# The rows that a piece of a DRAM-to-DRAM table copy takes: 128 in one stretch, or every 128th

## What is computed

```python
q = (ht @ w_q).reshape(-1, PEER_HEADS, PEER_QDIM)
s1, s2 = ...                                  # scores against two sets of 128 sub-keys
best, pos = lax.top_k(cand, PEER_TOPK)        # 8 heads x 16 experts
idx = jnp.take_along_axis(cidx, pos, axis=-1)
u = jnp.take(expert_u, ib, axis=0)            # rows of 1024 float32, 4 KB
act = jax.nn.gelu(jnp.einsum('td,tkd->tk', hb, u))
vrows = jnp.take(expert_v, ib, axis=0)
y = jnp.einsum('tk,tkd->td', gb * act, vrows)
```

## Time and profile before

| what | us |
|---|---|
| median of three runs (lowest, highest) | 4177.75 (4168.81, 4183.3) |
| the profiled execution | 4131.7 |
| its span in the trace | 4129.9 |
| last stage (gathers from `uv_d`), from about 1794 | some 2336 of the span |
| copy in stage A / B / E / S / P | 26 to 157 / 222 to 304 / 392 to 447 / 502 to 595 / 1241 to 1587 |
| TensorE, VectorE, GpSimd busy | 80%, 59%, 43% |
| bytes moved by DMA | 1563 MB, 378 GB/s over the span |

### The profile page before, as it was taken

How to read it: one execution, slowest core, us unless ns; L and a number is a source line. 1 busy time by engine, 2 the same in 40 slices (tenths; PEclk the granted TensorE clock), 3 DMA queues, 4 the chain that set the end, 5 groups by cost and what they waited for, 6 DMA issues and landing times.

```text
span 4129.9 us, 32128 instructions
## 1 busy us (share of the span) xinstructions
PE 3298.1 (80%) x8957; PEld 1643.4 (40%) x8957; DVE 2455.5 (59%) x4977; ACT 1088.2 (26%) x2932; POOL 1769.1 (43%) x1588
## 2 busy tenths in 40 slices
PE   8775589999928878749779779878878977977776
PEld 5453256666524444324224323323323423422222
DVE  0122168998857677544864764674684585485454
ACT  2102011111113233213333333333333333323322
POOL 1020137787723333114444454444444444445554
PEclk9876799999958888969999999999999999999999
DMA  9898899999999998469999999999999999999998
GB/s 352 297 290 310 321 304 413 411 407 414 412 360 341 344 354 300 160 269 420 421 421 418 415 420 399 421 414 409 420 409 409 419 417 403 422 406 422 422 422 353
DMA packets 303586, 1563.05 MB, mean 378 GB/s; under 512 B 31280, under 2 KB 59184, under 8 KB 179888
## 3 DMA queue, kind: packets, MB, share of 16 engines
q0 software_dynamic: 228096, 1300.34, 78.7%
q1 hardware_dynamic: 60736, 239.86, 15.0%
q10 hardware_dynamic: 14592, 21.10, 1.4%
HBM read 1517.54 MB, written 179.04 MB: 411 GB/s over the span
## 4 chain that ended last, share of the span: by engine, by line
DMA 26%; PE 18%; issue 7%; DVE 4%; ACT 1%; POOL 1%; POOLq 0%; ACTq 0%; DVEq 0%
DMA ring<-uv_d,IXD_p 26%; PE ps L1807 14%; PE ps L1779 3%; DVE ring L1906 2%; ACT dg L1850 1%; DVE BV_p L979 1%; POOL ring L2012 1%; ACT GE_p L1844 0%; DVE BP_p L984 0%; DVE CA_p L989 0%; DVE VV_p L1332 0%; DVE CA_p L1397 0%; DVE DOT_p L1906 0%; DVE ACC L1887 0%; PE ps L1796 0%
## 5 line engine op out<-in xcount | busy, mean ns | idle before, releaser
L1807 PE MATMUL ps<-ring,dg 128*128 128x512 f32 x3584 | 1704.6, 614 | 474.3 <-ACT dg L1850 449.9
L2012 POOL DMA_INDIRECT ring<-uv_d,IXD_p x896 | 1082.3, 1208 | 1318.1 <-PE ps L1807 1068.0
L1906 DVE CUSTOM_DVE_ANT_0 ring<-ring,H 128x1024 f32<-128x1024 f32 x896 | 1094.2, 1223 | 907.3 <-DMA ring<-uv_d,IXD_p 886.6
L1807 PEld LDWEIGHTS ps<-ring,dg 128*128 128x128 f32 x3584 | 664.0, 194 | 1432.8 <-ACT dg L1850 714.3
L1238 PE MATMUL ps<-w,xg 128*128 128x368 f32 x1792 | 554.3, 472 | 2.0 <-ACT SC_s L936 2.0
L1844 ACT ACTIVATE GE_p<-DOT_p 128x2 f32<-128x2 f32 x448 | 91.1, 203 | 1502.6 <-DVE DOT_p L1906 1502.6
L1238 PEld LDWEIGHTS ps<-w,xg 128*128 128x128 f32 x1792 | 340.4, 190 | 215.5 <-ACT SC_s L936 2.2
L1850 ACT ACTIVATE dg<-gdi,GE_p 128x128 f32<-128x128 f32 x896 | 310.6, 393 | 46.6 <-ACT GE_p L1844 1.2
L1838 ACT ACTIVATE gdi<-ident,GD_p 128x128 f32<-128x128 f32 x896 | 303.1, 386 | 26.3 <-issue 19.9
L145 POOL DMA_DIRECT2D uv_d<-in_peer_u x88 | 45.6, 518 | 504.7 <-DMA uv_d<-in_peer_v 270.3
L1779 PE MATMUL ps<-wq,hT_p 128*128 128x512 f32 x384 | 197.9, 597 | 0.0
(11 more groups left out here) (415 smaller groups left out, 2901.7 us busy)
## 6 DMA issues: line engine op xcount, KB each, us to landing
uv_d<-in_peer_u POOLq DMA_DIRECT2D x88, 512.0 KB, 5.4
uv_d<-in_peer_v POOLq DMA_DIRECT2D x88, 512.0 KB, 6.6
w<-in_w_in SPq DMA_DIRECT2D x8, 2944.0 KB, 15.1
w<-in_w_in SPq DMA_DIRECT2D x16, 1472.0 KB, 9.8
z_d<-zo ACTq DMA_DIRECT2D x16, 1288.0 KB, 18.8
uv_d<-in_peer_u SPq DMA_DIRECT2D x40, 512.0 KB, 9.6
uv_d<-in_peer_v SPq DMA_DIRECT2D x40, 512.0 KB, 11.3
ring<-uv_d,IXD_p POOLq DMA_INDIRECT x896, 11.2
```

What stands on the lines that cost most here:

```text
L1807: mm = T.matmul(bank(6 + n), dg[:, k % DR, :], ring[:, k % RS, D + n * 512:D + (n + 1) * 512], start=(k == 0), stop=(k == NK - 1))
L1906: V.tensor_tensor_reduce(out=row, in0=row, in1=H2[:], scale=1.0, scalar=0.0, op0=ALU.mult, op1=ALU.add, accum_out=DOT[:, k:k + 1]).then_in ...
L2012: g.indirect_dma_start(ring[:, n % RS, :], None, uv_d, bass.IndirectOffsetOnAxis(ap=IXD[:, n:n + 1], axis=0)).then_inc(s_ring[n % RS], 16)
```

## The change

`spread(table, part)` views a table as 128 runs of 128 rows and takes row `part` of each run. A piece is then the rows `part`, `part` + 128, `part` + 256 and so on up to `part` + 16256. It is used on both sides, in `pool_table` and in `rest_of_table`.

```diff
+        PIECES = NEXP // P
+
+        def spread(table, part):
+
+            return table.rearrange("(p n) d -> n p d", n=PIECES)[part]
+
...
-                g.dma_start(uv_d[part * P:(part + 1) * P, 0:D], rows(t["peer_u"], part)).then_inc(s_uv[part % 2], 16)
-                g.dma_start(uv_d[part * P:(part + 1) * P, D:], rows(t["peer_v"], part)).then_inc(s_uv[part % 2], 16)
+                g.dma_start(spread(uv_d, part)[:, 0:D], spread(t["peer_u"], part)).then_inc(s_uv[part % 2], 16)
+                g.dma_start(spread(uv_d, part)[:, D:], spread(t["peer_v"], part)).then_inc(s_uv[part % 2], 16)
...
-                sp.dma_start(uv_d[part * P:(part + 1) * P, 0:D], rows(t["peer_u"], part)).then_inc(s_uvs, 16)
-                sp.dma_start(uv_d[part * P:(part + 1) * P, D:], rows(t["peer_v"], part)).then_inc(s_uvs, 16)
+                sp.dma_start(spread(uv_d, part)[:, 0:D], spread(t["peer_u"], part)).then_inc(s_uvs, 16)
+                sp.dma_start(spread(uv_d, part)[:, D:], spread(t["peer_v"], part)).then_inc(s_uvs, 16)
```

## The result

The changed kernel takes 4318.3 us (median of four runs, 4288.27 to 4336.51) against 4180.52 us before, a ratio of 1.034 with a 95% interval of 1.029 to 1.038. On another chip, later, the same pair gave 4275.78 against 4168.97 us, 1.025 (1.021 to 1.029). The forecast was 4184 with a range up to 4300. The change costs 107 to 138 us. The first chip's time lies above the range, the second chip's inside it.

The account below looks back on a forecast made before the run. The last stage's gathers, untouched, take over half the span; only the copy before it can move. At +3% per packet, S 1.6, B 1.8, E 0.5, P 1.7, A 0 sum to 5.6, about 6 us: 4177.75 + 6 = 4184, range 4160 to 4300.

Parts of the forecast that it names:

- The part that bounds, and what can move: Last stage, gathering from `uv_d`, is over half the span and stays unchanged; only what lies before 1794 us can move.
- How many per cent a packet is longer: Copy packets in all five copy stretches: +3% on 210 ns, nothing for reads, a little for writes.
- The bounds: Copy packet time: from the gathers' 163 ns, 22% below 210, up to a factor of two from the worst slices.
- What 1% is worth: Us lost per 1% longer copy packet in each of five stretches; at +3% together 5.6 us.
- S: Stage S, copy directly ahead of gathers: 0.93 us for 1% after 1.2 us in hand; 1.6 us at +3%.
- B: Stage B, copy beside the load of `wo_s`: 0.6 us for 1%, at most about 13; 1.8 us at +3%.
- E: Stage E, POOL 11 us in hand: 0.15 us for 1% up to 10%, 0.55 beyond; 0.5 at +3%.
- P: Stage P, 40 pieces copied beside gathers: half of 1.14 taken, 0.55 us for 1%; 1.7 us at +3%.
- A: Stage A, 22 us in hand behind PE: nothing up to 17%, 1.3 us for each 1% beyond; 0 at +3%.
- The first rival: Copy writes queue where low address bits agree: +8 to +40%; at +20% 51 us, 4229; chance 0.26.
- the second rival: Same write queueing at its hardest, copy packets twice as long: 387 us more, about 4565; chance 0.10.
- The third rival: Copy gets faster because side-by-side rows slow it now: packets at 163 ns, 16 us gained, 4161; chance 0.12.

Follow-up runs that it names:

- (128,129): Copy alone, 16 pieces, reading every 128th row and writing with one spare row behind every 128, against every 128th on both sides: 62.8 us instead of 90.8.

## Why the prediction was wrong, point by point

**The part that bounds, and what can move.** Right. The last stage is 2334.4 and 2334.9 us, the packets are as many to one, the issue costs 0.52 us, and everything happened before 1794 (1994 after).

**How many per cent a packet is longer.** This step failed: "I take +3% for the copy packet: nothing for the reads, a little for the writes." It was 54% in stage E (210 to 323 ns) and 50% in stage S (214 to 320). The bounds held it, -22% to a factor of two, though the upper one was misread: the earlier trace rows has slices of 57 and 98 GB/s, under the 126 that was taken for the worst. Within the bounds I went by two rows of reads and said myself that neither had sixteen engines stepping through addresses that agree in their low bits. Both were loads into SBUF, and such loads lose 5% even at distance 128. The page of the Trainium skill that spoke against the change ("DMA: Bandwidth & Descriptors", "Latency and other measured facts") was right in direction. The estimate of 3 to 30% that was worked out from it was too mild for these pieces. Its observation that 4 KiB more between rows at 4 MiB restores the rate agrees in kind with (128,129), where 8 KB more at 1 MB makes 62.8 us of 90.8. "Nothing for the reads" was off as well, by less: the copy with only its reads apart lasted 10% longer by itself (66.6 for 60.6 us) and 13% in stage S, which came to 1.004 in time.

**What 1% is worth.** At +54% the terms of the prediction give S 50 - 1.2 = 49, B its cap of 13, E 1.5 + 24 = 26, P 30, A (54 - 17) x 1.3 = 48, together 166 us. The traces gave 92, 26, 31, 24 and 26, together 198. That the sums lie so close is partly luck, as the terms show:

- S: 58 us from the later first gather against 49. The packets took 50% longer and the copy 65% (93 to 153 us), because its tail now lies beside the projection's loads and stores: queues 1 and 10 moved 5.4 MB during the copy instead of 1.1. Missing were the us behind the first gather, 33 in the first pair of traces and some 20 by all of them. The prediction named what the late gathers wait for, but not who waits for the gathers: ACT, in the middle of emptying PE's banks.
- B: the cap was wrong. PE's wait for `wo_s` grew from 5.45 to 24.9 us, as the copy (its last piece issued at 381.93) outlived the whole load. The other 6 us are the store of `h_d`, for which SP waits at the stage's end: it landed 8.9 us behind its issue instead of 2.7.

```profile
PE ps L346 <- DMA wo_s<-in_w_out: 24.9, 1, 24.9
```

- A and E: the time in hand was misjudged. The part ahead of the prediction says that a piece need not have landed when a stage ends. The traces show otherwise. POOL closes each stage with a DRAIN; in stages A, B and E of both traces it ended 1.3 to 2.0 us behind the landing of POOL's last piece, and no engine started the next stage before that. Line, count, ns (shortest, median, longest) and start, for the ends of A and E, first before and then after:

```profile
L160 POOLq DRAIN  x1: 10148/10148/10148, 156.5 to 156.5; - x1
...
L819 POOLq DRAIN  x1: 10042/10042/10042, 446.5 to 446.5; - x1
```

```profile
L166 POOLq DRAIN  x1: 14342/14342/14342, 190.6 to 190.6; - x1
...
L825 POOLq DRAIN  x1: 11512/11512/11512, 528.6 to 528.6; - x1
```

- A: 26 against 48. Before, the DRAIN ended at 166.6 and SP, the last to arrive, was done at 179.2: 12.6 us in hand, not 22. After, it ended 38.3 us later, at 204.9, and 38.3 - 12.6 are the 25.7 us of the table. The 54% was too much here: next to the loads of `w_in` the packets took 32% longer and the copy lasted 26% longer. Two errors in opposite directions.
- E: 31 against 26. Before, the DRAIN ended at 456.6 and SP was done at 458.2: 1.6 us in hand, not 11. Counted from the stage's start it ended 32.2 us later after the change, and 32.2 - 1.6 is the stage's 31. PE's wait for `wq_s`, 37.0 us before, is 66.5 now:

```profile
PE ps L913 <- DMA wq_s<-in_peer_w_q: 66.5, 1, 66.5
```

  It is the same loss and not another one: from the start of stage S to PE's first matmul there the loads took 25.8 and 25.4 us.
- P: 24 against 30, and this is luck. Queue 1, which carries SP's copies and other loads, took 22% longer for 4 KB (175 to 213 ns), for which 0.55 us for 1% would give only 12. DVE's waits for gathers rose from 29.1 + 18.6 to 52.8 + 29.4. So 1% was worth about twice what was taken.

**The rivals.** The first rival named the right condition, addresses that agree in low bits, on the written side above all, with a price between its +40% and the second's factor of two. That the writes queue on few places of the memory is not shown: no run looks behind the addresses. I had given the two 0.36 together and the forecast 0.52. The range ended at the first rival's +40%, and the second rival was left out of it. The third rival's idea, that rows side by side are not the best pattern, also holds: at 127, 112, 32 and 16 the copy takes 54.4 to 55.5 us for 60.6. Its limit held too: a copy that is 8 to 10% faster gave 0.4%. The gathers of stage S left hardly earlier (595.86 against 597.44), since the indices are next, as was said.

## What to carry to other kernels

When a change keeps every count and alters only which addresses are in flight together, the trace before can bound the cost but not place it: a copy of a few pieces, alone, at each distance (60 us each) settles it at once, and should come before the rewrite. Between rows that are copied DRAM to DRAM, avoid 1 MB in the destination; one spare row behind every 128, or every 127th row in place of every 128th, is enough. Reckon the slack of a stage from the landing of the last DMA that POOL has issued in it, not from its issue. And a queue whose last transfer and first dependent gather are 1 us apart has no slack: what comes behind it starts late, and an engine with a fixed order of work across both streams, as ACT here, can pass the delay on to a third.

## What was not expected of the hardware

- The same set of rows costs the same in two quite different orders (90.1 and 89.6 us), and the cost is nearly absent with SBUF on one side (loads 50.8 and 53.3 us, stores 46.5 and 48.0).
- Reading every fourth row of 4 KB is slower (72.4 us for 16 pieces) than every 16th (60.6) or all of them (58.6); why is open.
- A copy of rows side by side is not the fastest: written every 16th row it took 53.6 us for 58.6.
- The DRAIN with which POOL closes a stage lasts until its copies have landed (10.1 us before and 14.3 after in stage A), so a copy that nobody reads yet can hold up every engine.
- The kernel before took 4133.6 us on one chip, 4167 to 4169 on three others and 4180.5 in the first job.
